# Modulation blocks of the feed-forward summed on VectorE alone, turned by a shifted column of ones, and collapsed by groups

## What is computed

```python
cond_lat = jax.nn.silu(c)[:, None, :]
cond_ctx = jax.nn.silu(c_ctx)[None, None, :]
for i in range(DEPTH):                                   # DEPTH = 2
    sh1, sc1, g1, sh2, sc2, g2 = jnp.split(cond_lat @ w_ada[i] + b_ada[i], 6, axis=-1)
    csh1, csc1, cg1, csh2, csc2, cg2 = jnp.split(cond_ctx @ w_ada[i] + b_ada[i], 6, axis=-1)
    h_lat = modulate(rms_norm(x, norm_gain[i, 0]), sh1, sc1)
    ...
    x = x + g1 * o_lat
    x = x + g2 * swiglu(modulate(rms_norm(x, norm_gain[i, 1]), sh2, sc2), ffn_w_in[i], ffn_w_out[i])
```

## Time and profile before

| | |
|---|---|
| median of 3 runs | 2472.69 us (2472.55 to 2476.56) |
| the profiled execution | 2477.41 us |
| its span | 2475.3 us |
| TensorE busy | 2404.4 us, 97% |
| VectorE busy | 1298.8 us, 52% |
| ScalarE, POOL busy | 879.4 us, 374.9 us |
| mean granted clock of TensorE | 0.994 |

### The profile page before, as it was taken

How to read it: one execution, slowest core, us unless ns; L and a number is a source line. 1 busy time by engine, 2 the same in 40 slices (tenths; PEclk the granted TensorE clock), 3 DMA queues, 4 the chain that set the end, 5 groups by cost and what they waited for, 6 DMA issues and landing times.

```text
span 2475.3 us, 34710 instructions
## 1 busy us (share of the span) xinstructions
PE 2404.4 (97%) x14354; PEld 2009.5 (81%) x14354; DVE 1298.8 (52%) x2101; ACT 879.4 (36%) x1499; POOL 374.9 (15%) x301
## 2 busy tenths in 40 slices
PE   8999999999999999999999999999999999999999
PEld 6778888888887777656888887988989878877788
DVE  3775625543535776875333336366565445554433
ACT  4331211111224444444222224364545333444422
POOL 0210000000014444501000001143343410000000
PEclk9999999999999999999999999999999999999999
DMA  9834334434321111012333332221222121121222
GB/s 324 204 94 125 119 103 130 126 119 118 104 68 35 52 38 48 35 44 76 92 96 102 95 93 86 69 69 52 69 69 78 60 69 52 52 69 52 77 94 111
DMA packets 252744, 220.79 MB, mean 89 GB/s; under 512 B 7480, under 2 KB 243443, under 8 KB 252204
## 3 DMA queue, kind: packets, MB, share of 16 engines
q1 hardware_dynamic: 249072, 217.92, 28.7%
q10 hardware_dynamic: 3260, 0.58, 0.1%
q0 software_dynamic: 256, 0.07, 0.0%
HBM read 214.26 MB, written 6.29 MB: 89 GB/s over the span
## 4 chain that ended last, share of the span: by engine, by line
PE 59%; ACT 3%; DVE 3%; issue 2%; POOL 1%; DVEq 0%; ACTq 0%; POOLq 0%
PE two L685 10%; PE bank L1354 5%; PE bank L1545 4%; PE bank L685 4%; PE bank L1350 3%; PE bank L1331 3%; PE two L1285 3%; PE bank L1526 2%; PE bank L1051 2%; PE two L1156 2%; PE bank L1182 2%; PE two L1565 2%; PE bank L1021 1%; PE bank L1033 1%; PE two L1297 1%
## 5 line engine op out<-in xcount | busy, mean ns | idle before, releaser
L2568 DVE TENSOR_TENSOR wL<-ring,wH 128x512 fp32r<-128x512 f32 x224 | 182.5, 829 | 225.3 <-ACT wH L1840 225.1
L1831 ACT ACTIVATE wH<-ring 128x2048 fp32r<-128x2048 f32 (+1 forms) x80 | 149.1, 1864 | 272.4 <-PE bank L690 73.4
L2557 DVE TENSOR_TENSOR wL<-ring,wH 128x2048 fp32r<-128x2048 f32 (+1 forms) x80 | 180.4, 2255 | 82.2 <-ACT wH L1831 82.0
L685 PE MATMUL two<-h1H,wH 128*128 128x512 f32 x496 | 195.5, 394 | 0.0
L685 PE MATMUL two<-h1H,wL 128*128 128x512 f32 x496 | 193.4, 390 | 0.0
L685 PE MATMUL two<-h1L,wH 128*128 128x512 f32 x496 | 193.3, 390 | 0.0
L1840 ACT ACTIVATE wH<-ring 128x512 fp32r<-128x512 f32 x224 | 133.6, 623 | 58.8 <-PE bank L1331 21.1
L1909 ACT ACTIVATE gateS<-two 128x512 f32<-128x512 f32 x44 | 26.3, 598 | 332.2 <-PE bank L690 142.0
L2661 DVE SCALAR_TENSOR_TENSOR xT<-two,ada,xT 128x512 f32<-128x512 f32 (+1 forms) x48 | 30.6, 679 | 186.2 <-PE bank L690 66.3
L3204 POOL TENSOR_TENSOR rstd<-rstd,sq 128x768 f32<-128x768 f32 (+1 forms) x15 | 30.4, 2024 | 611.4 <-ACT sq L1867 610.2
L1354 PE MATMUL bank<-unH,wH 128*128 128x272 f32 (+1 forms) x368 | 112.2, 305 | 3.9 <-ACT cin L2100 2.1
(11 more groups left out here) (642 smaller groups left out, 6953.5 us busy)
## 6 DMA issues: line engine op xcount, KB each, us to landing
ring<-in_ffn_w_in SPq DMA_DIRECT2D x88, 512.0 KB, 5.1
ring<-in_w_in SPq DMA_DIRECT2D x40, 1024.0 KB, 5.0
ring<-in_w_ada SPq DMA_DIRECT2D x32, 1024.0 KB, 5.2
ring<-in_ffn_w_out SPq DMA_DIRECT2D x16, 1024.0 KB, 5.1
early<-in_w_ada SPq DMA_DIRECT2D x12, 1024.0 KB, 12.0
ring<-in_diff_w_in SPq DMA_DIRECT2D x12, 1024.0 KB, 5.2
ring<-in_w_proj_ssd SPq DMA_DIRECT2D x8, 1024.0 KB, 4.9
ring<-in_ffn_w_out SPq DMA_DIRECT2D x8, 768.0 KB, 4.5
```

Source lines behind the costliest of these rows:

```text
L685: m = nc.tensor.matmul(bank[3 * s + half], w, r[:, 0:LAT], start=i == 0, stop=i == n - 1)
L1831: nc.scalar.activation(hi, raw, ACT.Copy).then_inc(w_hi, 1)
L2557: nc.vector.tensor_tensor(lo, raw, hi.bitcast(F32), ALU.subtract).then_inc(w_lo, 1)
L2568: nc.vector.tensor_tensor(lo, raw, hi.bitcast(F32), ALU.subtract).then_inc(q_lo, 1)
```

## The change

- The opening has 12 blocks instead of 16; 36 are left for later.
- `condz` is 62 columns wide for each chunk, zero but for the two conditions at 30 and 31. By taking its 32 columns from `30 - 2 * j` on, block j of a group lands on rows 2j and 2j+1 of the bank, so that a group is accumulated in one bank and is copied, turned and added to the bias once (`rows_of`, `sums_out`, `cols_of`, `take_ada`). `sel` becomes a 32-column selector. The groups are 8 and 4 blocks in the opening and 8 beside FNet's tiles.
- The other 28 blocks are all sums on VectorE beside the units of the first feed-forward. Two matmuls with a shifted column of ones (`onew`) as stationary of 32 columns and the 256 sums as the moving side put them on row j of two strips (`sums_of`); these are collapsed by groups of 4, 16 and 8.
- `stream_plan`: the block that is summed at unit u stands behind unit u+1 in the stream, before it stood behind unit u+2.
- Around this: `keep_busy(3, 4)` before the features, `keep_busy(2, 5)` instead of 4 before FNet's tiles, the first split of FNet's weights earlier on ScalarE and VectorE, all four foldings on POOL, and `take_ada(2)` behind `split_lo(5)` before the first norm.

```diff
@@ -28,7 +28,7 @@
-FRONT = 16
+FRONT = 12
...
-    for c in range(2):
-        k[c::32, K_SEL + c] = 1.0
+    k[:, K_SEL:K_SEL + 32] = i[:, None] % 32 == i[None, 0:32]
...
-ADA0 = [4, 5, 6, 7, 0, 1, 2, 3] + list(range(8, FRONT))
+ADA0 = list(range(FRONT))
 MORE = [("ada", 0, b) for b in range(FRONT, 24)] + [("ada", 1, b) for b in range(24)]
-BESIDE_ADA = [("fnet", cb) for cb in range(4)]
-BESIDE_ADA += sum([[("in", 0, c) for c in range(lo, hi)] + [("down", 0, lo, cb) for cb in range(4)] for lo, hi in GROUPS], [])
-STRIPS = [j for j, key in enumerate(BESIDE_ADA[:len(MORE)]) if j < 5 or key[0] == "down"]
-SUMS = [j for j in range(len(MORE)) if j not in STRIPS]
-ROWS_AT, COLS_AT = {1: [0], 3: [1], 5: [2], 6: [3]}, {2: [0], 4: [1], 6: [2], 7: [3]}
+UNITS0 = sum([[("in", 0, c) for c in range(lo, hi)] + [("down", 0, lo, cb) for cb in range(4)] for lo, hi in GROUPS], [])
+ADA_GROUPS = [[("ada", 0, b) for b in range(8)], [("ada", 0, b) for b in range(8, FRONT)], MORE[0:8], MORE[8:12], MORE[12:28], MORE[28:36]]
+SUMMED = MORE[8:]
+ROWS_AT = {0: [0], 1: [1], 2: [2], 3: [3], 4: [4, 5], 5: [6], 6: [7]}
...
-    plan = [("ada", 0, b) for b in ADA0]
-    plan += [("fnet", 0), ("fnet", 1), ("fnet", 2), MORE[0], ("fnet", 3)] + MORE[1:4]
+    plan = [("ada", 0, b) for b in range(FRONT)]
+    plan += [("fnet", 0), ("fnet", 1), ("fnet", 2), MORE[0], ("fnet", 3)] + MORE[1:8]
+    for u, unit in enumerate(UNITS0):
+        plan += [unit] + (MORE[6 + u:7 + u] if u >= 2 else [])
     for layer in range(2):
-        late = []
-        for lo, hi in GROUPS:
-            units = [("in", layer, c) for c in range(lo, hi)] + [("down", layer, lo, cb) for cb in range(4)]
-            for unit in units:
-                plan += [unit] + late
-                late = []
-                if layer == 0 and unit != ("in", 0, 0):
-                    late = MORE[BESIDE_ADA.index(unit) - 1:BESIDE_ADA.index(unit)]
+        if layer:
+            for lo, hi in GROUPS:
+                plan += [("in", 1, c) for c in range(lo, hi)] + [("down", 1, lo, cb) for cb in range(4)]
         if layer == 0:
             plan += DIFF
...
-        condz = sb("condz", [P, KC, 32])
+        condz = sb("condz", [P, KC, 62])
+        onew = sb("onew", [P, 63])
...
+            if key in SUMMED:
+                return ada_acc, SUMMED.index(key) + 1
             if key in MORE:
-                j = MORE.index(key)
-                return (ada_row, FRONT + STRIPS.index(j) + 1) if j in STRIPS else (ada_acc, SUMS.index(j) + 1)
+                return ada_row, FRONT + MORE.index(key) + 1
...
-                return (0, 1, NR, NR + 2, NR + 1, NR + 2, NR, NR + 2)[n - FRONT]
-            return n % (NR + 4) if n < 12 else NR + n - 12
+            return (0, 1, 2, 3, 4, 5, 0, 1, 2, 4, 3, 5, 0, 1, NR, NR + 2, NR + 1, 0, 1, NR + 2, NR, 0, 1, NR + 2)[n]
...
-            def ada_rows(i):
-
-                w = weights(("ada", 0, ADA0[i]))
-                if i >= 2:
-                    pe.wait_ge(ada_ev, i - 1)
-                else:
+            def rows_of(key):
+
+                w = slot(N_OF[key])
...
                 for kc in range(KC):
                     q = 32 * (kc % 4)
-                    m = nc.tensor.matmul(bank[4 + i % 2][q:q + 32, 0:256], condz[:, kc, :], w[:, kc, :], start=kc < 4, stop=kc >= 4)
+                    m = nc.tensor.matmul(bank[(4, 5, 7)[g]][q:q + 32, 0:256], condz[:, kc, 30 - 2 * j:62 - 2 * j], w[:, kc, :],
+                                         start=j == 0 and kc < 4, stop=last and kc >= 4)
                 m.then_inc(ada_row, 1)
 
-            def ada_cols(i):
...
+            def sums_of(key):
+
+                i = SUMMED.index(key)
+                g = [key in group for group in ADA_GROUPS].index(True)
+                j, last = ADA_GROUPS[g].index(key), key == ADA_GROUPS[g][-1]
+                pe.wait_ge(ada_acc, i + 1)
+                if j == 0:
+                    pe.wait_ge(ada_taken, g - 1)
+                for c in range(2):
+                    m = nc.tensor.matmul(bank[7 - g % 2][32 * c:32 * c + 32, 0:256], onew[:, 31 - j:63 - j], adacc[:, i % 2, c, :],
+                                         start=j == 0, stop=last)
                 m.then_inc(ada_row, 1)
 
-            def strip_cols(j):
-
-                pe.wait_ge(ada_ev, FRONT + STRIPS.index(j) + 1)
+            def cols_of(g):
+
+                pe.wait_ge(ada_ev, g + 1)
+                if g >= 3:
+                    for h in range(2):
+                        o = 256 + 64 * h
+                        m = nc.tensor.transpose(bank[7 - g % 2][:, o:o + 64], adrow[0:64, P * h:P * h + P], ident[0:64, 0:64])
+                    m.then_inc(ada_done, 1)
+                    return
                 for h in range(2):
-                    m = nc.tensor.matmul(bank[6 + j % 2][:, 256 + 2 * h:258 + 2 * h], adacc[:, j % 2, 0, P * h:P * h + P], sel,
+                    m = nc.tensor.matmul(bank[6 + g % 2 if g < 2 else 7 - g % 2][:, 256 + 32 * h:288 + 32 * h], adacc[:, g % 2, 0, P * h:P * h + P], sel,
                                          start=True, stop=True)
                 m.then_inc(ada_done, 1)
...
-                if j - 1 in STRIPS and j > 4:
-                    strip_rows(j - 1)
+                u = UNITS0.index(key)
+                for g in (3, 4, 5):
+                    if u == MORE.index(ADA_GROUPS[g][-1]) - 4:
+                        cols_of(g)
+                if 3 <= u < len(MORE) - 5:
+                    sums_of(MORE[5 + u])
...
-                    pe.wait_ge(ada_taken, FRONT + 4)
+                    pe.wait_ge(ada_taken, 3)
...
             for g in range(KC):
                 dft_rows(g)
                 if g == 1:
                     turned_columns()
                 if g == 2:
-                    pe.wait_ge(s_cols, 7)
                 for i in ([], [], [0], [1], [2, 3], [4], [5, 6], [7])[g]:
                     ada_rows(i)
-                    if i:
-                        ada_cols(i - 1)
-            ada_cols(7)
             for kc in range(4):
                 x_turned(kc)
-                ada_rows(8 + kc)
-                if kc:
-                    ada_cols(7 + kc)
+                if kc == 0:
+                    cols_of(0)
+            keep_busy(3, 4)
             for p in range(4):
                 dft_features(p)
-                ada_rows(12 + p)
-                ada_cols(11 + p)
+                ada_rows(8 + p)
             dft_middle()
-            ada_cols(FRONT - 1)
+            cols_of(1)
...
-            keep_busy(4, 5)
+            keep_busy(2, 5)
...
                     for j in ROWS_AT.get(m, ()):
-                        strip_rows(j)
-                    for j in COLS_AT.get(m, ()):
-                        strip_cols(j)
+                        rows_of(MORE[j])
+            cols_of(2)
...
+            split_hi(0)
             for kc in range(4, KC):
                 turned_ctx(kc)
-            split_hi(0)
...
+            def sums_out(g):
+
+                dve.wait_ge(ada_row, sum(len(x) for x in ADA_GROUPS[:g + 1]))
+                if g >= 3:
+                    dve.wait_ge(ada_done, g)
+                    nc.vector.tensor_copy(adrow[:], bank[7 - g % 2][0:64, 0:256]).then_inc(ada_ev, 1)
                     return
+                if g == 2:
+                    dve.wait_ge(ada_done, 1)
+                nc.vector.tensor_copy(adacc[:, g % 2, 0], bank[(4, 5, 7)[g]][:, 0:256]).then_inc(ada_ev, 1)
+
+            def take_ada(g):
+
...
+                o = 48 * layer + 2 * b
+                bias = colB[:, o:o + 2 * n].rearrange("p (j h) -> p j h", h=2).unsqueeze(3).broadcast_to([P, n, 2, 2])
+                nc.vector.tensor_tensor(ada[layer][:, 2 * b:2 * b + 2 * n, :].rearrange("p (j h) c -> p j h c", h=2), src, bias, ALU.add) \
+                    .then_inc(ada_taken, 1)
...
+            def sum_ada(key):
+
-                dve.wait_ge(ada_done, FRONT + b - 1)
+                if i < 2:
+                    dve.wait_ge(ada_done, 3)
+                else:
+                    dve.wait_ge(ada_row, FRONT + 8 + i - 1)
...
+            def more_sums(key):
+
+                if key not in UNITS0:
+                    return
+                u = UNITS0.index(key)
+                for g in (3, 4, 5):
+                    if u == MORE.index(ADA_GROUPS[g][-1]) - 5:
+                        sums_out(g)
+                    if u == MORE.index(ADA_GROUPS[g][-1]) - 4:
+                        take_ada(g)
+                if 1 <= u < len(MORE) - 7:
+                    sum_ada(MORE[7 + u])
...
                 layer, w = i // 2, i % 2
-                dve.wait_ge(ada_taken, 24 * layer + 12 * w + 8)
+                dve.wait_ge(ada_taken, (1, 3, 5, 6)[i])
...
-            take_ada(7)
+            rows_lo(3, 0, NT)
+            rows_lo(3, NT, 6)
+            lambdas()
+            sums_out(0)
+            take_ada(0)
             multipliers(0)
             for p in range(4):
                 scaled_rows(p)
                 turned_lat(p)
```

(29 more changed lines are left out.)

144 lines of the change are left out of this document (42 added, 102 removed).

## The result

The changed kernel takes **2519.27 us** (median of 4 runs, 2518.48 to 2522.51), the kernel before 2472.62 beside it (2472.09 to 2476.56): 1.0184 times as long, 95% interval 1.0171 to 1.0196. It is slower, as forecast, but by 46.7 us where 8.4 were forecast, and the time lies above the range of 2456 to 2496.

The account below looks back on a forecast made before the run. TensorE, busy 97%, was taken as the bound, with a loop through SP making it wait in the first feed-forward: -3.8 before the first unit's end plus 12.2 gives +8.4 on 2472.7, so 2481.1 us, range 2456 to 2496.

Parts of the forecast that it names:

- the loop: First feed-forward: sum, SP issue, landing, high and low part repeat every 18.85 us ("in") or 18.25 ("down"), above TensorE's 17.35.
- the path from the last sum to the end of the feed-forward: End of the first feed-forward: unit 31 waits 7.8 us for its slot and weights, then three units of 12.5 follow.
- beyond 740 us nothing: After the first feed-forward the change does nothing, as the stream and its two slots are the same.
- the opening: Before FNet: -7.6 us until the eighth block's rows, -0.2 to the features, -1.9 in them, -1.6 from `keep_busy`.
- the landing: Feed-forward: a block and the unit's weights behind it land in 8.5 us for "in" units, 7.9 for "down".
- rival 3: First feed-forward: landings of 9.0 and 8.5 end at 2495 us, or late `hidL` costs some 2 us twice; chance 0.15.
- The Trainium skill's fit: Feed-forward weights: 2.0 us plus bytes over 436 GB/s gives 6.8 us for both transfers, a loop of 17.2, no TensorE wait.
- `hidL` behind a late sum: First feed-forward: the last "in" unit's `hidL` holds up the first "down" unit, some 2 us each time, twice.
- TensorE's own work: First feed-forward: `sums_of` at 0.65 us each makes 553.4 us against 565.2, 11.8 won if TensorE sets the pace.
- rival 4: Feed-forward: if the two strips run one behind the other, `sums_of` costs 0.9 us; no chance of its own.
- folding moves to POOL; it is hidden: Before FNet: folding its first weight block on POOL is hidden, because these weights are issued some 15 us earlier.
- The first norm: Norm sums wait for the low part, +2.2 us, idle about 3; half clock adds 2.1; +4.3 together.

Follow-up runs that it names:

- late_block: Changed kernel with each summed block back behind unit u+2 in the stream, as before the change; 2479.64 us.
- late_placed: late_block plus unused stretches of 64 and 832 bytes, putting `h1` and `hid` 2048 bytes further on than before the change; 2469.03 us.
- placed_after: Changed kernel with its own stream order and only the two unused stretches of late_placed (64 and 832 bytes); 2510.88 us.
- spare64_before: Kernel before with 64 unused bytes ahead of `ring`, `wH`, `wL`, `h1` and `hid`; 2472.65 us.
- late_placed_fold: late_placed with folding of FNet's first weight block back on VectorE and the first high part behind the turned context rows; 2461.75 us.
- place512_before: Kernel before with 512 unused bytes in each partition behind `condz`; 2471.24 us (one run).
- place1152_before: Kernel before with 1152 unused bytes behind `condz`, putting `h1`, `hid` and `gateS` where the changed kernel has them; 2489.29 us.
- half_block: Changed kernel transferring only four of eight chunks of each block summed in the first feed-forward; 2481.02 us.

## Why the prediction was wrong

The direction was right; the time was 38 us too low. Four steps failed: the length of the loop, the path from the last sum to the end of the feed-forward, "beyond 740 us nothing", and the opening. Between the two profiles, whose spans differ by 40.8 us, this is where the forecast's 8.4 fell short:

| | forecast, us | measured, us |
|---|---|---|
| shift of the first silu | -3.8 | 0.0 |
| 26 rounds of the loop | 485.3 | 498.7 |
| from the last sum's end to the last unit's end | 45.3 | 53.3 |
| change behind the first feed-forward | 0 | +7.5 |

By the medians of the runs the changed kernel's loss comes apart so: the stream's order 39.6, the place of `h1` and `hid` 10.6, folding and addition together 10.2 (7.3 and 4.7 alone), and against them 14.5 gained by all the rest. These are the steps of one chain of kernels, so their sum, 45.9 for 46.7, is no check of them. In another order they differ: the place alone gives 8.4 on the changed kernel, and the order 41.9 after it.

- **The bound, and where to look.** Right: TensorE's waits in the first feed-forward carry most of it.
- **The loop.** Right in its mechanism and its place: SP's two issues stand together, ScalarE's high part waits for the DMA, silus go from 17.6 apart (224.91 to 242.51) to 17.7 to 21.0, 19.3 on average, from the 14th unit on, and the first sum ends 29.7 us after the first silu (forecast 29.8). Mis-sized in one term, the landing: 8.5 and 7.9 us were taken, 9.0 and 8.4 measured on average, which are the 9.0 and 8.5 of rival 3. The upper bound ("can't be later than 8.9") was no bound: 9.91 occurred. In the row it came from, the block had a head start of 3 us and the halves' issue took 0.99 us; here the halves' issue takes 1.9 to 2.4. Which of the two makes the difference is open. All else in the round is as forecast (10.28; 453.59 less 443.28 is 10.31). 26 rounds at 19.18 for 18.67 are 13.4 us.
- **The Trainium skill's fit** for the pair, 6.8 us, was rightly set aside: no round has it; the shortest landing of a block and a full unit behind it is 8.1. The page gives that fit for DMAs that GpSimd issues; these are SP's.
- **`hidL` behind a late sum** was in rival 3 with twice 2 us. It came three times, 2.00, 3.68 and 4.47. The first two fall within rounds of the loop that are no longer than the others (18.68 and 18.52 us), so they cost TensorE time that it would have waited anyway. The last one sets the end: the forecast let the last slot decide, with 7.8 us and three units (45.3) behind the last sum; in the trace the gate product and `hidL` come behind that sum (720.19 to 723.04) and four units behind them (to 773.49), 53.3. So the step is worth 8.0 us, and it belonged into the sum, not among the rivals.
- **The clock.** The same loss seen from TensorE: 29.7 us of idle time and the 9.2 us of matmuls at half clock, less 5.2 by which its own work got shorter (late_block's first feed-forward against before's), make 33.7 for the 33.3 measured. As the loop sets the pace until the last sum, only the last group at half clock (2.0 us) lies on the path to the end.
- **TensorE's own work** there: `sums_of` was taken at 0.65 with its change of unit. In late_placed, where the place of `h1` is as before, silus with a sum are 17.45 apart and without 16.68: 0.77. The gain, forecast 11.8, is 8.9 (563.65 for 572.51). From its first matmul to the next unit's it takes 0.56 us. The trace has four records for it, two to a strip; the 16 of `strip_rows`, four to a strip, take 1.00, so 0.25 each on their strip. One behind the other the four would take 1.00. So the two strips run beside each other, and rival 4 is out.
- **"Beyond 740 us nothing."** Wrong, and no rival had it: 7.2 us by the profiles behind the third rstd, 10.4 to 11.0 against the old program's profiles whose clock didn't dip there (1344.6 for 1334.2 and 1333.6). placed_after gives back 8.4 by the medians. The cause lies in three tile sizes (`condz`, `onew`, `cond`) that the prediction didn't cost at all.
- **The opening.** The eighth block's row ends at 53.6 (forecast 54.6), the features start at 65.82 (66). Then "folding moves to POOL; it is hidden" failed: FNet starts 4.4 us later than forecast, and late_placed_fold, with the folding back, starts it 5.9 earlier. It looked only at whether the weights had landed, not at what GpSimd's work does to VectorE's beside it. FNet itself took 4.7 us more for 3.2; a part of its first matmuls is at half clock (0.69 from 92.5 to 98). The 2.2 us for the half clock at 44 are a gain in some executions only: in the four profiles of the old program the clock from 44 to 48 is 0.50, 1.00 (spare64_before), 0.75 (place512_before) and 0.50 (place1152_before), and FNet starts at 95.5 to 97.8 in the three others, not at 99.47.
- **The first norm.** The wait was right: the sums start 5.5 us after FNet's last matmul where it was 3.3, idle 3.04 (forecast about 3), +2.2. The 2.1 us for the clock didn't come between these two profiles: from the sums' start to the first silu it is 27.9 us in both, as the kernel before was in part at half clock a little later (0.66 from 153 to 158). Against the 26.1 to 26.2 of the three other profiles of the old program they did come.
- **The median.** 4.7 us were taken off for what the profiled execution had over the median. The changed kernel's own profiled execution lies 0.8 under its median, so 5.5 us more stand between the two medians than between the two profiles.

## What to carry to other kernels

When a transfer is put in a queue behind one whose slot comes free late, follow its consumer on: if it leads back to what frees the slot, the loop's length is the period, and every 0.1 us counts once per round. Then ask what comes behind the last round in program order. A change of tile sizes moves every tile behind it: compare the pitch of matmuls that the change doesn't touch, before looking for another reason. Work moved from VectorE to GpSimd wasn't hidden here, because VectorE was on the path beside it.

## What was not expected of the hardware

- The pitch of fp32r matmuls with 512 moving columns went with the place of the tiles `h1`, `hid` and `gateS`: 0.227 us with `h1` and `hid` at 192 or 256 bytes past a multiple of 512, 0.233 at 320 or 384, with no other change in the program (spare64_before, place512_before, place1152_before). Shifting the stationary tile by 64 bytes did nothing.
- GpSimd's additions stretch VectorE's from 1.22 to 3.37 us, and a 16-column operation from 0.18 to 1.60.
- Two DMA issues of 512 KB took SP 1.9 to 2.4 us behind a megabyte issued 0.4 us before (18 pairs of the changed kernel, 2.23 at 434.81), 1.1 to 1.5 behind half a megabyte (half_block), and 0.99 to 1.00 where 2.6 us or more lay between (the kernel before, late_block).
